# The split weight tiles of a one-core kernel placed behind the activations in SBUF

## The chip, the cores and the metric

One NeuronCore of a Trainium2 chip. The metric is the device time of one execution in microseconds (us); the median of three runs stands for a kernel.

## The reference, cut to what matters

Four residual half blocks and then a second block work on x, 256 tokens by 1024 features, in float32. What counts here is that nearly all of it is products of activations with weight matrices that are each used once:

```
h = rms_norm(x, g0);  x = x + rms_norm(mlstm_mixer(h), g1)        # w_in 1024 -> 3080, w_out 1024 -> 1024
h = rms_norm(x, g2);  x = x + rms_norm(relu(h @ w_up)**2 @ w_down, g3)   # 1024 -> 4096 -> 1024
... the same with short_conv_mixer (w_in 1024 -> 3072), and a second up/down
second block: x = x + [retention, pooling](norm(x) @ w_in) @ w_out
              x = x + softmax(q k^T / 16) v @ wo      # k, v from mem, 256 tokens by 1024
              x = x + (silu(gate) * val) @ w_down     # gate, val = conv3(norm(x) @ w_up), 1024 -> 5632, 2816 -> 1024
return rmsnorm(x, final_norm_g)
```

## The kernel before, in words

**Layout.** Activations are kept transposed: features on the 128 partitions, 8 chunks of them, 256 tokens along the free axis. Weights come from HBM as 159 slabs of 1 MB, each 128 x 2048 floats: 8 blocks of input features times 256 output columns.

For full precision each operand is split in a high part and a remainder: wH, wL for weights, xnH, xnL (normed activations), memH, memL (memory tokens), hH, hL (hidden layer of the MLPs) and mixH, mixL (mixer output) for activations. A product is three matmuls (`products`, L416 to L421): wH with the high activations, wH with the remainder, wL with the high ones. Per slab that is 8 blocks x 2 halves of columns x 3 = 48 matmuls, each 128 x 128 loaded against 128 x 256 streamed. The weight tile is the loaded operand, the activations stream:

```
pe.matmul(psum[:, n, 0:T], wH[w][:, wc], aH[:, ac, :], start=start, stop=False)     # L419: loads wH, streams aH
pe.matmul(psum[:, n, 0:T], wH[w][:, wc], aL[:, ac, :], start=False, stop=False)     # L420
return pe.matmul(psum[:, n, 0:T], wL[w][:, wc], aH[:, ac, :], start=False, stop=stop)  # L421
```

In ten slabs (v, rv and the fillers f4 to f7; `slab_by_token`, L438 to L448) it is the other way round: a 128 x 128 tile of the activations is loaded and 256 columns of wH or wL are streamed, so that tokens come out on partitions. In the names of the trace, `po<-xnH,wL` streams xnH and loads wL, and `po<-wL,xnH` streams wL and loads xnH.

**The stream of slabs.** SyncE loads slab s into raw[s % 4] as soon as the split of slab s - 4 is finished (`load`, L378). ScalarE copies each half slab to wH[s % 2] (`split`, L805), rounding it; VectorE writes wL = raw - wH (L1245), 318 instructions each. The write of wH for slab s waits until TensorE has finished the same half of slab s - 2. TensorE waits for each half's wL.

**The order of the work** is written out by hand in `PHASES` (L51): qk, v, o, out0, f4, f0, up0 (16 slabs), down0 (16), f1, cin (12), out1, f5, f2, up1, down1, f6, f3, rq, ru, rv, rg, out2, wq, f7, wo, fup (22), fdown (11). Where no number stands it is 4 slabs, or 2 for ru, rv and rg, or 1 for f0 to f7. The f slabs are fillers: products of the memory tokens with the keys' and values' weights, put where TensorE would otherwise wait for a norm. out0, out1, out2 and wo stream mixH and mixL; down0, down1 and fdown stream hH and hL; f0 to f3 stream memH and memL; all other slabs but the by-token ones stream xnH and xnL. Between the slabs' products TensorE does small work in plain fp32: sums of squares for the norms (L487), their spread over partitions (L494), head scores (L510, L511), attention scores (L721) and values (L743).

**The places in SBUF.** `sb` (L96) gives each tile the next free byte of every partition, in steps of 32, starting at the first multiple of 64 that is free (L94); in the program built here this is byte 16512, which is 128 past a multiple of 512. All residues in this document are counted mod 512 from that first byte, the start of raw0. The order of before is:

| tiles | bytes per partition | residue of each |
|---|---|---|
| raw0 to raw3 | 4 x 8192 | 0 |
| wH0, wH1, wL0, wL1 | 4 x 8192 | 0 |
| x, xnH, xnL, memH, memL, memk, memv | 7 x 8192 | 0 |
| ident, ones | 2 x 512 | 0 |
| par | 1312 | 0 |
| Rs, Rm, diag | 3 x 1024 | 288 |
| warm, ms, minus_half, rtok, rmem | 5 x 32 | 288 and up |
| scratch (y, squares, hrelu, hsq, apad, cgate, ...) | 16384 | 448 |
| region: hH, hL (32768 each), or mixH, mixL, qT, kT, xq, ... | | 448 for hH, hL, mixH, mixL, qT, kT, xq and xpT |

Every chunk of an activation tile is 1024 bytes and every block of weights 512, so each operand of a product starts at its tile's residue.

Of the kernel before, what the change touches and what calls it, by code (L numbers as in the profile page):

```python
# [2 lines left out]

# [6 lines left out]
P = 128  # L25
T = 256
TT = T // P
# [17 lines left out]
SLAB = 16 * P  # L45
HALF = SLAB // 2
RAW = 4
HL = 2
# [39 lines left out]
def build(nc, xT, memT, pos, weights, wgate, params, poolw, tri, mask, select, decay, freq, recount, out):  # L88
    f32, f32r, i32 = mybir.dt.float32, mybir.dt.float32r, mybir.dt.int32
# [3 lines left out]
    with ctx:  # L93
        place = [nc.sbuf_base + (-nc.sbuf_base) % 64]  # L94

        def sb(name, shape, dt, at=None):  # L96
            size = int(np.prod(shape[1:])) * 4
            if at is None:
                off = place[0]
                place[0] += (size + 31) // 32 * 32  # L100
            else:
                off = at[0]
                at[0] += (size + 31) // 32 * 32
            return nc.alloc_sbuf_tensor_at(name, list(shape), dt, offset=off)
# [3 lines left out]

        raw = [sb(f"raw{i}", [P, SLAB], f32) for i in range(RAW)]  # L110
        wH = [sb(f"wH{i}", [P, SLAB], f32r) for i in range(HL)]
        wL = [sb(f"wL{i}", [P, SLAB], f32r) for i in range(HL)]
        x = sb("x", [P, C, T], f32)
        xnH = sb("xnH", [P, C, T], f32r)
        xnL = sb("xnL", [P, C, T], f32r)
# [4 lines left out]
        ident = sb("ident", [P, P], f32)  # L120
        ones = sb("ones", [P, P], f32)
        par = sb("par", [P, NPAR], f32)
        Rs = sb("Rs", [P, T], f32)
        Rm = sb("Rm", [P, T], f32)
        diag = sb("diag", [P, TT, P], f32)
        warm = sb("warm", [P, 1], f32)
        ms = sb("ms", [P, TT], f32)
        minus_half = sb("minus_half", [P, 2 * NH], f32)
        rtok = sb("rtok", [P, TT], f32)
        rmem = sb("rmem", [P, TT], f32)  # L130
        scratch = place[0]
        at = [scratch]
        y = sb("y", [P, C, T], f32, at)
# [1882 lines left out]
```

## Time and profile before

| | |
|---|---|
| median of 3 runs | 1009.82 us (1009.44 to 1010.5) |
| span of the profiled execution | 1008.9 us, mean granted clock of TensorE 0.993 |
| TensorE busy (matmul, weight load) | 974.7 us (97%), 961.8 us (95%) |
| VectorE, ScalarE, POOL busy | 657.2 us (65%), 536.5 us (53%), 191.0 us (19%) |
| read from HBM | 170.24 MB |

The profile has the span alone (first to last instruction of one execution); its own total time is not recorded beside it, so the span stands against the median of the three other runs. Busy time of TensorE is of overlapping matmuls: a matmul's duration contains its way through the array, and the next one starts long before its end. A pace is therefore read from starts in the timeline.

### The profile page before, as it was taken

Reading aid. Unit: us, or ns where it says so; the run is one execution under the profiler, and the core shown is the slowest. Engines: PE = TensorE matmul, PEld = TensorE weight load, DVE = VectorE, ACT = ScalarE, POOL = GpSimd, SP = SyncE. Lnnn points to the kernel's source line nnn. Section 1 sums busy time; section 2 is a strip of 40 time slices with the busy share of each in tenths; the row PEclk is TensorE's granted clock in tenths of the full one; section 3 lists DMA queues with packets and bytes.
Section 4 is the critical chain, followed back from the end, with each engine's and each line's share of the span. In section 5 each row is a group of like instructions: output and inputs, shape, how many; then the busy total and the mean of one; then the engine's idle time right before and its main releaser. Section 6 shows DMA issues by size and latency. Waiting matters only on the chain.

```text
span 1008.9 us, 20181 instructions
## 1 busy us (share of the span) xinstructions
PE 974.7 (97%) x8062; PEld 961.8 (95%) x8062; DVE 657.2 (65%) x843; ACT 536.5 (53%) x754; POOL 191.0 (19%) x159
## 2 busy tenths in 40 slices
PE   7999989999999899999999999989999999999996
PEld 6999989999999799989999999889999999999995
DVE  6567586665444876577665444874865779999642
ACT  5566646554443544556555444554554566666541
POOL 2021140000010400149000010455120122223101
PEclk9999999999999999999999999999999999999997
DMA  9533635555555354535555553544342545555521
GB/s 342 183 126 112 216 131 188 190 171 204 186 189 172 123 206 168 189 129 190 196 173 198 182 205 137 196 159 168 128 166 86 181 152 177 197 191 183 205 88 42
DMA packets 25844, 172.17 MB, mean 171 GB/s; under 512 B 3252, under 2 KB 3892, under 8 KB 5432
## 3 DMA queue, kind: packets, MB, share of 16 engines
q1 hardware_dynamic: 25784, 171.30, 49.0%
q8 instruction: 46, 0.75, 0.3%
q14 instruction: 14, 0.11, 0.0%
HBM read 170.24 MB, written 1.05 MB: 170 GB/s over the span
## 4 chain that ended last, share of the span: by engine, by line
PE 85%; DVE 7%; issue 3%; POOL 2%; ACT 2%; DMA 1%; DVEq 0%; SPq 0%; ACTq 0%; POOLq 0%
PE po L419 25%; PE po L420 25%; PE po L421 25%; DVE xnL L1252 2%; DVE wL L1245 2%; PE po L446 2%; POOL rtok L1821 2%; PE po L448 2%; PE po L447 2%; PE pn L494 1%; ACT wH L805 1%; PE pn L487 1%; PE pc L743 1%; DMA raw<-in_weights 1%; DVE diag L1271 0%
## 5 line engine op out<-in xcount | busy, mean ns | idle before, releaser
L1245 DVE TENSOR_TENSOR wL<-raw,wH 128x1024 fp32r<-128x1024 f32 x318 | 404.0, 1294 | 157.8 <-ACT wH L805 157.8
L805 ACT ACTIVATE wH<-raw 128x1024 fp32r<-128x1024 f32 x318 | 334.8, 1059 | 295.5 <-PE po L421 264.8
L419 PE MATMUL po<-xnH,wH 128*128 128x256 f32 x1376 | 396.8, 288 | 18.9 <-DVE xnL L1252 13.2
L420 PE MATMUL po<-xnL,wH 128*128 128x256 f32 x1376 | 389.9, 283 | 0.0
L421 PE MATMUL po<-xnH,wL 128*128 128x256 f32 x1376 | 389.7, 283 | 0.0
L419 PEld LDWEIGHTS po<-xnH,wH 128*128 128x128 f32 x1376 | 264.3, 192 | 23.6 <-DVE xnL L1252 9.6
L420 PEld LDWEIGHTS po<-xnL,wH 128*128 128x128 f32 x1376 | 264.5, 192 | 0.2
L421 PEld LDWEIGHTS po<-xnH,wL 128*128 128x128 f32 x1376 | 264.4, 192 | 0.0
L419 PE MATMUL po<-hH,wH 128*128 128x256 f32 x688 | 189.9, 276 | 0.0
L420 PE MATMUL po<-hL,wH 128*128 128x256 f32 x688 | 189.9, 276 | 0.0
L421 PE MATMUL po<-hH,wL 128*128 128x256 f32 x688 | 189.9, 276 | 0.0
L1808 POOL TENSOR_TENSOR squares<-squares 128x512 f32<-128x512 f32 x26 | 39.7, 1528 | 525.0 <-ACT squares L853 368.7
L419 PEld LDWEIGHTS po<-hH,wH 128*128 128x128 f32 x688 | 129.1, 188 | 0.0
L420 PEld LDWEIGHTS po<-hL,wH 128*128 128x128 f32 x688 | 129.1, 188 | 0.0
L421 PEld LDWEIGHTS po<-hH,wL 128*128 128x128 f32 x688 | 129.1, 188 | 0.0
L419 PE MATMUL po<-mixH,wH 128*128 128x256 f32 x256 | 71.8, 280 | 0.5 <-DVE mixL L1287 0.5
L420 PE MATMUL po<-mixL,wH 128*128 128x256 f32 x256 | 71.0, 277 | 0.0
L421 PE MATMUL po<-mixH,wL 128*128 128x256 f32 x256 | 71.0, 277 | 0.0
L1512 DVE SCALAR_TENSOR_TENSOR hrelu<-po,Rs 128x512 f32<-128x512 f32 x32 | 22.1, 690 | 55.8 <-PE po L421 55.7
L1252 DVE SCALAR_TENSOR_TENSOR xnL<-x,par,xnH 128x256 fp32r<-128x256 f32 x56 | 48.6, 918 | 7.5 <-ACT xnH L819 7.5
L419 PEld LDWEIGHTS po<-mixH,wH 128*128 128x128 f32 x256 | 48.1, 188 | 0.9 <-DVE mixL L1287 0.7
L421 PEld LDWEIGHTS po<-mixH,wL 128*128 128x128 f32 x256 | 48.3, 189 | 0.0
(284 smaller groups left out, 1097.1 us busy)
## 6 DMA issues: line engine op xcount, KB each, us to landing
raw<-in_weights SPq DMA_DIRECT2D x158, 1024.0 KB, 4.8
x<-in_xT SPq DMA_DIRECT2D x4, 256.0 KB, 6.4
raw<-in_weights SPq DMA_DIRECT2D x2, 512.0 KB, 6.2
mem<-in_memT SPq DMA_DIRECT2D x1, 1024.0 KB, 12.6
out<-y SPq DMA_DIRECT2D x4, 256.0 KB, 2.4
decayt<-in_decay SPq DMA_DIRECT2D x1, 512.0 KB, 3.7
poolwt<-in_poolw SPq DMA_DIRECT2D x1, 256.0 KB, 3.7
par<-in_params SPq DMA_DIRECT2D x1, 164.0 KB, 3.4
```

What stands on the lines that cost most here:

```text
L419: pe.matmul(psum[:, n, 0:T], wH[w][:, wc], aH[:, ac, :], start=start, stop=False)
L420: pe.matmul(psum[:, n, 0:T], wH[w][:, wc], aL[:, ac, :], start=False, stop=False)
L421: return pe.matmul(psum[:, n, 0:T], wL[w][:, wc], aH[:, ac, :], start=False, stop=stop)
L446: pe.matmul(psum[:, t, 0:256], aH[:, k, tc], wH[w][:, wc], start=k == 0, stop=False)
L447: pe.matmul(psum[:, t, 0:256], aL[:, k, tc], wH[w][:, wc], start=False, stop=False)
L448: mm = pe.matmul(psum[:, t, 0:256], aH[:, k, tc], wL[w][:, wc], start=False, stop=k == 7)
L805: act.activation(wH[b % HL][:, hs], raw[b % RAW][:, hs], ACT.Copy).then_inc(s_hi, 1)
L1245: dve.tensor_tensor(wL[b % HL][:, hs], raw[b % RAW][:, hs], wH[b % HL][:, hs].bitcast(f32), ALU.subtract)\
L1252: k = dve.scalar_tensor_tensor(xnL[:, c, :], x[:, c, :], col(gain, c), xnH[:, c, :].bitcast(f32), ALU.mult, ALU.subtract)
L1512: dve.scalar_tensor_tensor(hrelu[n % 2][:, :, :], slot(GROUP0[up] + n)[:, :, 0:T], 0.0, over_pair(Rs[:, :]), ALU.max, ALU.mult).then_inc(s ...
L1808: pool.tensor_tensor(sq[0], sq[0], sq[p], ALU.add).then_inc(s_sqa, 1)
L1821: pool.tensor_tensor(r[:, :], ms[:, :], minus_half[:, 0:TT], ALU.pow).then_inc(s_r, 1)
```

## The change

The lines that allocate wH and wL move from behind raw to behind rmem, and Rs, Rm and diag move behind them. Nothing else in the program differs, apart from blank lines at the head of the file, which shift line numbers.

```
-        wH = [sb(f"wH{i}", [P, SLAB], f32r) for i in range(HL)]
-        wL = [sb(f"wL{i}", [P, SLAB], f32r) for i in range(HL)]
         x = sb("x", [P, C, T], f32)
...
         par = sb("par", [P, NPAR], f32)
-        Rs = sb("Rs", [P, T], f32)
-        Rm = sb("Rm", [P, T], f32)
-        diag = sb("diag", [P, TT, P], f32)
         warm = sb("warm", [P, 1], f32)
...
         rmem = sb("rmem", [P, TT], f32)
+        wH = [sb(f"wH{i}", [P, SLAB], f32r) for i in range(HL)]
+        wL = [sb(f"wL{i}", [P, SLAB], f32r) for i in range(HL)]
+        Rs = sb("Rs", [P, T], f32)
+        Rm = sb("Rm", [P, T], f32)
+        diag = sb("diag", [P, TT, P], f32)
         scratch = place[0]
```

Behind raw, whose end has residue 0, x to memv take 7 x 8192 bytes, ident and ones 1024, par 1312 and the five small tiles 160. So wH0 begins at residue 1024 + 1312 + 160 = 2496, which is 448 mod 512, and so do wH1, wL0, wL1, Rs, Rm and diag. x to par lie 32768 bytes lower, with the residues they had. The scratch and the region behind it stay at the same bytes.

| operands of the split products | slabs | loaded, streamed: before | after |
|---|---|---|---|
| weights loaded, xn or mem streamed | 90 | 0, 0 | 448, 0 |
| xn or mem loaded, weights streamed | 10 | 0, 0 | 0, 448 |
| weights loaded, hidden layer or mixer output streamed | 59 | 0, 448 | 448, 448 |

## Rows read from the trace of the kernel before

**Rows 1.** The page: span, busy time, and the chain that ended last by engine.
```profile
span 1008.9 us, 20181 instructions
PE 974.7 (97%) x8062; PEld 961.8 (95%) x8062; DVE 657.2 (65%) x843; ACT 536.5 (53%) x754; POOL 191.0 (19%) x159
...
PE 85%; DVE 7%; issue 3%; POOL 2%; ACT 2%; DMA 1%; DVEq 0%; SPq 0%; ACTq 0%; POOLq 0%
```

**Rows 2.** Waits: who waited for whom, us in total, times, longest us.
```profile
ACT wH L805 <- PE po L421: 264.8, 201, 4.4
...
PE po L419 <- DVE xnL L1252: 13.2, 11, 2.3
PE pn L494 <- DVE diag L1271: 3.9, 11, 1.6
```

**Rows 3.** Timeline of PE (start, us): a slab's ends in up1, down0, out2; v.
```profile
479.82 0.28 PE L419 MATMUL po<-xnH,wH 128*128 128x256 f32 x1
...
485.58 0.28 PE L419 MATMUL po<-xnH,wH 128*128 128x256 f32 x1
...
239.73 0.28 PE L419 MATMUL po<-hH,wH 128*128 128x256 f32 x1
...
245.17 0.28 PE L419 MATMUL po<-hH,wH 128*128 128x256 f32 x1
...
721.07 0.28 PE L419 MATMUL po<-mixH,wH 128*128 128x256 f32 x1
...
726.72 0.28 PE L419 MATMUL po<-mixH,wH 128*128 128x256 f32 x1
...
62.14 0.28 PE L447 MATMUL po<-wH,xnL 128*128 128x256 f32 x1
...
64.78 0.28 PE L448 MATMUL po<-wL,xnH 128*128 128x256 f32 x1
```

**Rows 4.** Windows (length, PE, PEld, DVE, ACT, POOL, PEclk): out0, up0, down0, fdown; fup's loop.
```profile
101.61:123.55 21.94, 21.94 (x196) 21.94 (x194) 13.33 (x14) 13.24 (x20) 3.33 (x3) 1.00 0.59 200
137.30:233.93 96.63, 94.27 (x778) 93.31 (x777) 63.81 (x73) 54.19 (x68) 7.69 (x6) 1.00 0.52 178
233.93:320.99 87.06, 87.06 (x771) 87.06 (x769) 41.78 (x35) 38.81 (x43) 3.33 (x3) 1.00 0.57 195
935.74:995.49 59.75, 59.75 (x530) 59.75 (x528) 28.76 (x29) 26.06 (x32) 5.94 (x5) 1.00 0.34 118
...
840.00:909.12 69.12, 69.12 (x579) 69.12 (x578) 66.72 (x86) 44.96 (x62) 18.66 (x14) 1.00 0.56 193
```

**Rows 5.** Groups by line and form: busy us, mean ns | idle before, releaser.
```profile
L1245 DVE TENSOR_TENSOR wL<-raw,wH 128x1024 fp32r<-128x1024 f32 x318 | 404.0, 1294 | 157.8 <-ACT wH L805 157.8
L421 PE MATMUL po<-xnH,wL 128*128 128x256 f32 x1376 | 389.7, 283 | 0.0
L421 PEld LDWEIGHTS po<-xnH,wL 128*128 128x128 f32 x1376 | 264.4, 192 | 0.0
L421 PE MATMUL po<-hH,wL 128*128 128x256 f32 x688 | 189.9, 276 | 0.0
L421 PEld LDWEIGHTS po<-hH,wL 128*128 128x128 f32 x688 | 129.1, 188 | 0.0
L420 PE MATMUL po<-memL,wH 128*128 128x256 f32 x64 | 18.1, 283 | 0.0
```

**Rows 6.** Small fp32 products: durations min/median/max ns by tile; the last from the timeline.
```profile
L510 PE MATMUL pc<-qT,kT x4: 377/377/378, 54.8 to 65.1; 128*128 128x256 f32 x4
L511 PEld LDWEIGHTS pc<-qT,kT x4: 188/188/189, 55.0 to 65.3; 128*128 128x128 f32 x4
L721 PE MATMUL pa<-memk,xq x16: 377/379/379, 752.7 to 766.0; 128*128 128x256 f32 x16
...
64.91 0.59 PE L510 MATMUL pc<-qT,kT 128*128 128x256 f32 x2
```

**Rows 7.** Groups of VectorE in fup's loop, 840 to 909.12 us.
```profile
L1245 DVE TENSOR_TENSOR wL<-raw,wH 128x1024 fp32r<-128x1024 f32 x26 | 39.4, 1554 | 0.0
```

## The prediction

> **What bounds the kernel now.** I read the page's busy shares first: TensorE works 97% of the span, VectorE 65%, ScalarE 53% [rows 1]. The chain that ended last agrees, with 85% of it on TensorE [rows 1], and TensorE's two largest sums of waits are 13.2 us, at the starts of stages whose activations are still being split, and 3.9 us [rows 2]. So the time is 7632 split products (159 slabs of 48), almost back to back, and the pace of one product decides. That pace can't be read from a mean duration, since matmuls overlap; the timeline gives it. From the first product of a slab to the first of the next there are 48 intervals: 485.58 - 479.82 = 5.76 us where xnH and xnL stream, 120.0 ns each; 245.17 - 239.73 = 5.44 us where hH and hL do, 113.3 ns [rows 3]. TensorE has the same granted clock, 1.00, in both stretches [rows 4], the same shapes and the same weight tiles. The groups by form repeat it: 283 ns for a matmul and 192 for a weight load with xn, 276 and 188 with hH [rows 5]. The by-token slabs, with activations loaded and weights streamed, also run at 120.0: 62.14 to 64.78 is 22 intervals [rows 3].
>
> What differs is the place. Residues below are mod 512 bytes, counted from the block's first tile. wH, wL, xnH, xnL, memH and memL lie at 0, while hH, hL, mixH and mixL lie at 448. So (loaded 0, streamed 0) costs 120.0 ns, (0, 448) 113.3, a difference of 6.67 ns. The four slabs of out2 are an exception: with (0, 448) they go at 726.72 - 721.07 = 5.65 us for 48, 117.7 ns, though out0 with the same tiles takes 21.94 us for 4 slabs, 5.49 each [rows 3, 4]. The pace then has at least three settled values, and residues alone don't choose between them.
>
> **The change part by part.** No instruction is added or removed, and no wait. (a) xnH, xnL, memH, memL streamed against weights now at 448: the pair is (448, 0), 4320 products in 90 slabs. (b) By-token slabs: (0, 448), the fast pair of today, 480 products in 10 slabs. (c) hH, hL, mixH, mixL: (448, 448), 2832 products in 59 slabs. (d) Rs, Rm and diag go from 288 to 448, and everything else keeps its residue. ScalarE writes and VectorE reads and writes the weight halves at another residue; the 318 splits of VectorE, 1294 ns each [rows 5], and as many copies of ScalarE have slack in all stages but one, where wH's next load waits 264.8 us in sum for TensorE [rows 2]. I cost (d) and this at nothing; without that cover each 10 ns on VectorE's 318 would be 3.2 us.
>
> The trace has no product with weights at 448, so I bound each pair from the nearest rows: 113.3 below and 120.0 above. The mechanism I take is that the two reads of TensorE disturb each other when both start at the same residue, and not otherwise: then (a) falls to 113.3, (b) as well, and (c) rises to 120.0. For: it is what separates the two populations, and the settled values hold for thousands of products whatever the other engines do. Against: the scores, both operands at 448, load kT in 188 ns at the median of L511 and stream in 377 [rows 6], no longer than memk at 0 against xq at 448 (379). But two of those products take 0.59 us from the first's start to the second's end [rows 6], so they start 0.59 - 0.38 = 0.21 us apart: longer than a load, which then bounds nothing, and they weigh little.
>
> Gain of (a) and (b), a slab giving 48 x 6.67 = 0.32 us where TensorE is never held:
> - up0, up1 and cin: 44 slabs, 14.1 us. VectorE is busy 63.8 of 96.6 us in up0 [rows 4], so it stays behind cover there; I keep 95%, 13.4.
> - fup: 22 slabs, 7.0 us at full rate. Here VectorE is busy 66.72 of 69.12 us, over 12 slabs [rows 4]: 5.56 us of work a slab, where TensorE would want 5.44. VectorE becomes the bound, and a slab saves 0.20 and not 0.32: 20 x 0.20 = 4.0, of which I take 3.0, since POOL's products (its tensor ops stretch the splits: 1554 ns here against 1294 overall [rows 5, 7]) come no sooner.
> - The other 34 slabs (qk, v, o, rq to rg, wq, and the eight fillers): 10.9 us at full rate. They hide norm chains, softmax and rotary work of the other engines, and a shorter cover leaves a longer wait behind it: the waits on xnL (11 of them, 13.2 us) and on diag (11, 3.9 us) [rows 2] would grow by what the slabs ahead save. I keep 60%, 6.5.
> Together 22.9 us, with 32.0 as upper end and some 16 (half) as lower.
>
> Loss of (c): down0, down1 and fdown are 43 slabs at 5.44 (59.75 / 11 = 5.43 [rows 4]), out0, out1 and wo 12, so 55 x 0.32 = 17.6; the 4 of out2 lose only 5.76 - 5.65 each, 0.4. TensorE is never idle there, so all 18.0 us count.
>
> Net -4.9 us on a span of 1008.9 [rows 1]. The three runs have a median of 1009.82, 0.9 us more than the profiled span, which I add: 1004.9, **1005 us**. The ends of this case are 1009.8 - 32.0 + 18.0 = 996 and 1009.8 - 16 + 18.0 = 1012.
>
> A rule speaks against any effect. The Trainium skill (SBUF — State Buffer, "Who interferes with whom") gives TensorE two independent read ports, one for the moving operand and one for weight loads, and says that TensorE never waits on anyone. By it placement is worth 0 and the sum stays 1009.8. Its sentence leaves 120.0 against 113.3 [rows 3] unexplained, so as far as it goes the trace does not agree.
>
> **The rivals.** What would measure as no change is within 0.2% (2.0 us).
> - *Settling between.* (a) ends in the 117.7 state of out2 [rows 3]: (c) costs 18.0, but (a) and (b) give 2.33 / 6.67 of 22.9, 8.0. 1009.8 + 10.0 = 1020, slower. For: fresh from a stop, that state caught (0, 448) once. Against: out0, with the same pair, runs at 5.49 us a slab [rows 4]. It turns slower as soon as the settled pace of (a) is above 114.8 ns (18.0 / 22.9 = 79% of 6.67 is needed to break even). 13%.
> - *One order only is good.* Fast needs the streamed tile 64 bytes behind the loaded one, as now with (0, 448); 64 ahead is as bad as level. (a) stays at 120.0, (c) rises by 18.0 us, and only (b) gains, 10 x 0.32 x 0.6 = 1.9: 1026, slower. 10%.
> - *Only the streamed tile's place counts.* 448 streamed is fast, whatever is loaded. (a) and (c) stay, (b) gains 1.9: 1008, on the edge of what can be measured. For: every fast product of the trace streams from 448, every slow one from 0, and kT's 188 ns with both at 448 [rows 6]. Against: no reason for a place to be bad by itself. 22%.
> - *The loaded tile at 448 is fast against anything.* (a) and (b) gain 22.9, (c) keeps 113.3: 987. Nothing in the rows has it but kT's 188 ns. 10%.
> - *Nothing.* High bytes or the tiles' history set the pace and the shift is empty: 1009.8. Against: memL lies 24 KB above xnH and has the same 283 ns [rows 5]. 5%. The rule of the Trainium skill named above leads here.
>
> **How the numbers follow.** The forecast has 40%. From it 33 points are faster, 5 within, 2 slower, since its own range runs from 996 to 1012. The streamed-place case splits 10 and 12, the loaded-place case is all faster (10), nothing is within (5), and the two slower cases are slower (23). Sum: faster 0.53, same 0.22, slower 0.25. The range runs from 998 to 1026; it leaves out the 987 case (10%) and the far end of the forecast.
>
> **What will show it.** Timeline of the profile after, 48 intervals of a slab: 5.44 us in up1 and 5.76 in down0 if I am right; by-token intervals at 113.3; fup at 5.55 to 5.6 a slab with VectorE busy 99% and TensorE waiting for wL; median loads 188 ns for xn and 192 for hH. Up at 5.76 and down at 5.44 would be the streamed-place case; up at 5.44 with down at 5.44 the loaded-place case; down at 5.76 without a gain in up one of the slower two. What would make me most wrong is a fourth settled value that (448, 0) has and no pair of today shows.

## The result: 0.6% slower, and the profile after

The kernel after takes 1016.0 us at the median of 9 runs (1013.10 to 1019.48), the kernel before 1009.91 in 9 runs beside it (1008.82 to 1012.91). The ratio is 1.0058, with a 95% interval of 1.0042 to 1.0075: slower, by nearly three times the 0.2% below which a difference would count as no change. The forecast was 1005 us, 0.5% faster.

The page of the kernel after: span, busy times of the engines, and the chain that ended last by engine.

```profile
span 1013.6 us, 20181 instructions
PE 980.2 (97%) x8062; PEld 967.2 (95%) x8062; DVE 660.7 (65%) x843; ACT 537.0 (53%) x754; POOL 187.7 (19%) x159
...
PE 84%; DVE 7%; issue 3%; POOL 2%; ACT 2%; DMA 1%; DVEq 0%; SPq 0%; ACTq 0%; POOLq 0%
```

Everything that [rows 1] showed is still so: the same number of instructions, the same busy shares, the same bound (TensorE has 84% of the chain in place of 85%). The span grew by 4.7 us. So the difference has to lie in the pace of the products. Below is the timeline of the kernel after, the two ends of one slab each in up0, down0, cin and up1 (columns: start us, duration us, engine, line, operation, tiles; 48 intervals lie between the two rows of a pair).

```profile
186.49 0.28 PE L404 MATMUL po<-xnH,wH 128*128 128x256 f32 x1
...
192.14 0.28 PE L404 MATMUL po<-xnH,wH 128*128 128x256 f32 x1
...
277.79 0.28 PE L404 MATMUL po<-hH,wH 128*128 128x256 f32 x1
...
283.55 0.28 PE L404 MATMUL po<-hH,wH 128*128 128x256 f32 x1
...
373.25 0.28 PE L404 MATMUL po<-xnH,wH 128*128 128x256 f32 x1
...
378.90 0.28 PE L404 MATMUL po<-xnH,wH 128*128 128x256 f32 x1
...
492.53 0.28 PE L404 MATMUL po<-xnH,wH 128*128 128x256 f32 x1
...
497.97 0.28 PE L404 MATMUL po<-xnH,wH 128*128 128x256 f32 x1
```

Down0 went from 5.44 to 5.76 us a slab, as forecast. Up0 and cin went from 5.76 only to 5.65, 117.8 ns a product, and up1 to the 5.44 that was forecast for all three, though it streams the same tiles against the same weights as up0. The stages tell the same in sum. Windows of the kernel after (length; busy us and count of PE, PEld, DVE, ACT, POOL; granted clock; DMA share; GB/s): out0, up0, down0, cin, up1, down1, fup, fdown, and the stretch in fup's loop.

```profile
99.64:122.86 23.22, 23.22 (x195) 23.16 (x194) 13.62 (x14) 13.50 (x20) 3.33 (x3) 1.00 0.56 195
136.48:231.71 95.23, 92.65 (x778) 91.67 (x777) 63.93 (x73) 54.27 (x68) 7.79 (x7) 1.00 0.53 180
231.71:323.87 92.16, 92.16 (x771) 92.16 (x770) 41.89 (x35) 38.72 (x43) 3.32 (x3) 1.00 0.54 186
333.57:407.17 73.60, 71.51 (x584) 71.01 (x585) 54.70 (x72) 37.14 (x49) 10.22 (x7) 0.95 0.47 160
443.55:536.05 92.50, 89.57 (x779) 88.61 (x777) 67.75 (x73) 54.44 (x69) 32.90 (x30) 1.00 0.54 184
536.05:628.20 92.15, 92.15 (x770) 92.15 (x769) 41.80 (x35) 40.73 (x46) 3.33 (x3) 1.00 0.49 169
810.43:937.24 126.81, 125.93 (x1066) 125.41 (x1065) 117.65 (x153) 81.43 (x111) 31.72 (x23) 1.00 0.52 179
937.24:1000.54 63.30, 63.30 (x530) 63.30 (x528) 30.48 (x33) 26.27 (x32) 5.92 (x5) 1.00 0.33 117
840.00:909.12 69.12, 69.12 (x590) 69.12 (x589) 67.38 (x88) 45.34 (x62) 17.78 (x12) 1.00 0.55 186
```

Against [rows 4], and against the same stages of before that no row there shows (up1 96.77, cin 74.56, fup 128.99, down1 87.06 us): down0 and down1 lose 5.1 each, fdown 3.6, the three outs and wo 1.3 + 1.1 + 0.4 + 1.1, together 17.6 us. Up0 gains 1.4, cin 1.0, up1 4.3, fup 2.2, v 1.1, and all the rest 2.9, together 12.9. The net is the 4.7 us by which the span grew; the 2.9 is what the other stages leave of it.

A part of cin's time is the clock's, whose mean is 0.95 there and 1.00 in the other stages. Windows of the kernel after over cin's start show where:

```profile
333.57:340.00 6.43, 4.58 (x23) 4.28 (x24) 6.43 (x9) 5.38 (x10) 4.75 (x4) 0.58 0.00 0
340.00:346.00 6.00, 6.00 (x49) 6.00 (x47) 3.48 (x4) 2.12 (x2) 3.85 (x3) 0.89 0.21 55
```

TensorE had waited 2.10 us for the split activations just ahead, and after its first products waits 1.85 more; the granted clock of 0.58 is mostly the lower level, 1.2 GHz, and from 346 us on it is 2.4 again. Before has a fall there too (0.98 over cin). At the lower level a product takes longer; these two rows of the kernel after have 15 intervals between them, 213.3 ns each:

```profile
337.89 0.41 PE L405 MATMUL po<-xnL,wH 128*128 128x256 f32 x1
...
341.09 0.41 PE L405 MATMUL po<-xnL,wH 128*128 128x256 f32 x1
```

Means over all products of a kind hide the two paces. Groups by form of the kernel after (count | busy us, mean ns | idle before):

```profile
L1230 DVE TENSOR_TENSOR wL<-raw,wH 128x1024 fp32r<-128x1024 f32 x318 | 411.1, 1316 | 168.6 <-ACT wH L790 168.5
L406 PE MATMUL po<-xnH,wL 128*128 128x256 f32 x1376 | 384.8, 280 | 0.0
L406 PEld LDWEIGHTS po<-xnH,wL 128*128 128x128 f32 x1376 | 260.0, 189 | 0.0
L406 PE MATMUL po<-hH,wL 128*128 128x256 f32 x688 | 194.7, 283 | 0.0
```

Against [rows 5], hH has taken the 283 ns that xnH had, and xnH has 280, between the 276 of hH and the 283 of xnH in the kernel before: a mixture. What TensorE waits for is hardly changed; waits of the kernel after (us in total, times, longest):

```profile
PE po L404 <- DVE xnL L1237: 12.6, 11, 2.1
PE pn L479 <- DVE diag L1256: 4.5, 11, 1.6
PE po L404 <- DVE wL L1230: 2.4, 3, 2.1
```

### The profile page after: what moved, and what is told of

The parts are those of the page before. It is cut to its first block, busy times and chain, and to the rows that moved or that the text cites. A ratio compares the mean times of both kernels' runs of the same rounds, so it can differ in the third digit from the quotient of the medians.

```text
span 1013.6 us, 20181 instructions
## 1 busy us (share of the span) xinstructions
PE 980.2 (97%) x8062; PEld 967.2 (95%) x8062; DVE 660.7 (65%) x843; ACT 537.0 (53%) x754; POOL 187.7 (19%) x159
## 4 chain that ended last, share of the span: by engine, by line
PE 84%; DVE 7%; issue 3%; POOL 2%; ACT 2%; DMA 1%; DVEq 0%; SPq 0%; ACTq 0%; POOLq 0%
PE po L404 25%; PE po L406 24%; PE po L405 24%; DVE xnL L1237 3%; DVE wL L1230 2%; PE po L431 2%; POOL rtok L1806 2%; PE po L432 2%; PE po L433 2%; PE pn L479 1%; ACT wH L790 1%; PE pn L472 1%; PE pc L728 1%; DMA raw<-in_weights 1%; DVE diag L1256 0%
## 5 line engine op out<-in xcount | busy, mean ns | idle before, releaser
L1230 DVE TENSOR_TENSOR wL<-raw,wH 128x1024 fp32r<-128x1024 f32 x318 | 411.1, 1316 | 168.6 <-ACT wH L790 168.5
L404 PE MATMUL po<-xnH,wH 128*128 128x256 f32 x1376 | 392.6, 285 | 17.7 <-DVE xnL L1237 12.6
L405 PE MATMUL po<-xnL,wH 128*128 128x256 f32 x1376 | 385.0, 280 | 0.0
L406 PE MATMUL po<-xnH,wL 128*128 128x256 f32 x1376 | 384.8, 280 | 0.0
L405 PEld LDWEIGHTS po<-xnL,wH 128*128 128x128 f32 x1376 | 259.9, 189 | 0.2
L406 PEld LDWEIGHTS po<-xnH,wL 128*128 128x128 f32 x1376 | 260.0, 189 | 0.0
L404 PE MATMUL po<-hH,wH 128*128 128x256 f32 x688 | 194.8, 283 | 0.0
L405 PE MATMUL po<-hL,wH 128*128 128x256 f32 x688 | 194.7, 283 | 0.0
L406 PE MATMUL po<-hH,wL 128*128 128x256 f32 x688 | 194.7, 283 | 0.0
L405 PEld LDWEIGHTS po<-mixL,wH 128*128 128x128 f32 x256 | 49.1, 192 | 0.0
```

Source lines behind the costliest of these rows:

```text
L1230: dve.tensor_tensor(wL[b % HL][:, hs], raw[b % RAW][:, hs], wH[b % HL][:, hs].bitcast(f32), ALU.subtract)\
```

## The experiments

In all that follows a pace is the mean time from the start of one product to the start of the next in a slab of 48, from the timeline; intervals of 130 ns and more (another product between, a wait) are left out. "Distance" is the residue of the streamed tile minus that of the loaded one, the shorter way round; a pair at distance 0 is called level. A "stop" is a place where TensorE starts no product for a while: it waits, or does small work of another kind in between. Before has distance 0 for xn and mem and -64 for h and mix; after has +64 and 0, and in its by-token slabs -64. Each kernel of this part was run with the kernel before beside it on the same chip, which took 1010.9 to 1011.3 us at the median. The ratios come from that comparison and are not exactly the quotient of the two medians.

**Is a level pair what costs, wherever the tiles lie?** Two kernels change the place of the scratch and of the region behind it alone, h and mix with them. The first starts from the kernel after; its h and mix go to residue 0 and so to +64:

```diff
+        place[0] += 64
         scratch = place[0]
```

> The changed kernel with 64 more bytes in front of the scratch: hidden layer and mixer output go from residue 448 to 0, weights stay at 448. Now both xn and h are streamed 64 bytes ahead (mod 512) of the loaded weights and nothing is level. Theory A (level start residues cost 120.0 ns a product; any other distance gives one of two settled paces, 113.3 or 117.8, picked at each stop of TensorE): the 59 slabs of h and mix leave 120.0 for a mixture of 113.3 and 117.8, so 6.5 to 18.9 us less than the 1016 of the changed kernel, 997 to 1010. Theory B (the order counts: 64 behind gives 113.3, 64 ahead 117.8): h and mix at 117.8 throughout, 1009 to 1010. Theory C (weights at 448 are slow against any tile but xn): h stays at 120.0 and the time at 1016.

Measured: 1011.52 us (999.79 to 1013.78, 10 runs), ratio to before 0.9981 (0.9949 to 1.0012). The 17.6 us are not all won back, because h and mix went from 120.0 to 117.8 and not to 113.3, in all seven stages. (Only the first 36 products of out1, entered from cin without a stop, held cin's 113.3; from the first stop on out1 too was at 117.8.) Timeline, a slab of down0 and one of cin:

```profile
277.39 0.28 PE L405 MATMUL po<-hH,wH 128*128 128x256 f32 x1
...
283.04 0.28 PE L405 MATMUL po<-hH,wH 128*128 128x256 f32 x1
...
369.65 0.28 PE L405 MATMUL po<-xnH,wH 128*128 128x256 f32 x1
...
375.09 0.28 PE L405 MATMUL po<-xnH,wH 128*128 128x256 f32 x1
```

Cin, untouched by this edit, ran at 113.3 here where the kernel after had 117.8. The second kernel does the same to the kernel before, so that h and mix are at distance 0 with the weights at their old place:

```diff
+        place[0] += 64
         scratch = place[0]
```

> The kernel before with 64 more bytes in front of the scratch and nothing else: hidden layer and mixer output go from residue 448 to 0, level with the weights at 0. This is the loss part of the change alone, at another absolute place. Theory A and B: 59 slabs at 5.76 us, 120.0 ns a product and the same in every execution, 18.3 us more than before, 1028. Theory C (it was the weights' place 448, not the distance, that slowed h): 113.3 stays, 1010. In between would speak against all three.

Measured: 1028.18 us (1027.20 to 1028.77, 4 runs), ratio 1.0176 (1.0159 to 1.0193). All stages settle at 120.0. Timeline, a slab of down0:

```profile
281.39 0.28 PE L420 MATMUL po<-hH,wH 128*128 128x256 f32 x1
...
287.15 0.28 PE L420 MATMUL po<-hH,wH 128*128 128x256 f32 x1
```

The same step of 64 bytes costs 1.76% in one kernel (1011.0 to 1028.2 us at the median) and wins in the other, where the ratio to before falls from the 1.0064 of the kernel after in this comparison (the next run) to 0.9981, and the median by 4.6 us. So neither a tile's own place nor a place of the loaded tile decides whether a pair is slow, but the distance. And distance 0 is at 120.0 in every stage of every profile: the loss of (c) is real and has this cause.

**Was 117.8 a matter of one execution?** The kernel after, unchanged, once more:

> The changed kernel once more, for a second profile of the same program. Theory A: h and mix at 120.0 again in every slab, but the stages of xn that sat at 113.3 (up1) and at 117.8 (up0, cin, fup) are others this time, and the time moves with them between 1013 and 1020. Theory B and any theory in which addresses alone choose the pace: up1 at 113.3 and up0, cin, fup at 117.8 again.

Measured: 1016.10 us (1012.44 to 1018.97, 4 runs), ratio 1.0064 (1.0041 to 1.0087), profiled span 1010.1. Timeline, a slab of cin:

```profile
370.96 0.28 PE L404 MATMUL po<-xnH,wH 128*128 128x256 f32 x1
...
376.40 0.28 PE L404 MATMUL po<-xnH,wH 128*128 128x256 f32 x1
```

Up0 is at 117.8 again, cin now at 113.3: its stage took 69.98 us, not 73.60, of which 12 slabs x 48 x 4.5 ns = 2.6 is the pace, and the granted clock is 1.00 over cin here in place of 0.95. The same program has another pace in the same stage. Those 3.6 us make up the difference of the two spans (3.5); fup won another 1.1 us (125.7 for 126.8), as its slabs 3 to 9 were at 113.3 here until a stop of 0.24 us at the start of slab 10 brought 117.8, and fdown lost the 1.1 again.

**Does the order count?** The kernel before with its small tiles moved ahead of x, so that x, xn and mem come to 448 with h and mix, and the weights stay at 0: every product by features is at -64, the by-token ones at +64.

```diff
+        ident = sb("ident", [P, P], f32)
+        ones = sb("ones", [P, P], f32)
+        par = sb("par", [P, NPAR], f32)
+        warm = sb("warm", [P, 1], f32)
...
         x = sb("x", [P, C, T], f32)
```

> The kernel before with ident, ones, par and the five small tiles allocated ahead of x: x, xn and mem go to residue 448, where h and mix are already, weights stay at 0. All 149 slabs that load weights stream 64 bytes behind them; the ten by-token slabs stream 64 ahead. Theory B: 113.3 nearly everywhere (out2's 117.8 an exception), VectorE bound in fup, about 22 us less than before, 987. Theory A: 113.3 in some stages and 117.8 in others, as the stops have it: between 987 and 1002 (all at 117.8 would save 8), and different from run to run by some us. If one order were bad by itself, as the rival of the prediction had it, xn at 64 behind would still give 987.

Measured: 1001.33 us (998.76 to 1011.16, 10 runs), ratio 0.9916 (0.9889 to 0.9943). It is faster than before, since nothing is level. Yet -64 is not simply the fast one: up0 went at 117.8 (95.2 us for the stage), and so did down0; fup was at 113.3 for 17 slabs and at 117.8 for its last five, again from a stop on. Timeline, a slab each of down0 and up1:

```profile
276.38 0.28 PE L419 MATMUL po<-hH,wH 128*128 128x256 f32 x1
...
282.03 0.28 PE L419 MATMUL po<-hH,wH 128*128 128x256 f32 x1
...
486.55 0.28 PE L419 MATMUL po<-xnH,wH 128*128 128x256 f32 x1
...
491.99 0.28 PE L419 MATMUL po<-xnH,wH 128*128 128x256 f32 x1
```

Down0 of this kernel has the pair that took 87.06 us before, and took 90.5. What differs is what came ahead: before, TensorE entered down0 without a stop from level products at 120.0; here it entered from up0 at 117.8, and stayed there. So, where nothing stops TensorE and the distance stays the same, the pace goes over from one stage to the next. In the kernel before, all of out1, down0, down1 and fdown were entered from level products without a stop, and all four settled at 113.3. The third value that out2 of before had [rows 3] is the same 117.8, there taken up right behind a stop.

**Which distances?** Four kernels shift x and everything behind it in the kernel before by one line ahead of x:

```diff
+        place[0] += 256
         x = sb("x", [P, C, T], f32)
```

and the same with 128, 32 and 192.

> The kernel before with 256 bytes left free between wL and x: weights at 0, xn and mem at 256, hidden layer and mixer output at 192. Theory A (only level is slow, every other distance has the same two paces): no 120.0 anywhere, stages at 113.3 or 117.8 as the stops have it, so 997 to 1005 and a spread of several us between executions, like the kernel with the activations at 448. Theory D (the distance sets more than level or not): one pace throughout, either 113.3, which gives 987 with VectorE bound in fup, or another value than the three known.

Measured: 1010.98 us (1010.16 to 1012.45, 10 runs), ratio 1.0002 (0.9991 to 1.0012). Timeline, a slab of up0 and one of down0:

```profile
187.59 0.28 PE L420 MATMUL po<-xnH,wH 128*128 128x256 f32 x1
...
193.35 0.28 PE L420 MATMUL po<-xnH,wH 128*128 128x256 f32 x1
...
277.21 0.28 PE L420 MATMUL po<-hH,wH 128*128 128x256 f32 x1
...
282.65 0.28 PE L420 MATMUL po<-hH,wH 128*128 128x256 f32 x1
```

At 256 the old picture is back, 120.0 and 113.3, so distances count mod 256 and not mod 512: 256 acts as level, and 192, where h and mix are now, acts as -64 did.

> The same with 128 bytes: xn and mem at 128, hidden layer and mixer output at 64. Theory A: 113.3 or 117.8 in every stage, 997 to 1010. Theory D: xn at a pace of its own, and h (64 ahead) at 117.8 as with the scratch moved by 64, so the two kinds of stages differ in a fixed way.

Measured: 1017.77 us (1016.07 to 1020.70, 4 runs), ratio 1.0054 (1.0035 to 1.0073). Here xn is at 128 and goes at 118.7 in most stages and at 120.0 in up0 and fup; h and mix at +64 go at 117.8 in all.

> The same with 32 bytes: xn and mem at 32, hidden layer and mixer output at 480, 32 behind. It asks how wide level is. If two reads disturb each other only when they start at the same residue, 32 is as good as 64: 113.3 or 117.8, 997 to 1010. If what they share is a unit of 64 bytes or more, xn at 32 stays level with weights at 0 and costs 120.0 (90 slabs), while h at 480 lies in the unit behind and keeps 113.3: 1008 to 1011, as before.

Measured: 1013.64 us (1012.56 to 1014.88, 10 runs), ratio 1.0025 (1.0015 to 1.0035): xn at +32 at 116.7, in fup at 117.8; h and mix at -32 at 118.3.

> The kernel before with 192 bytes between wL and x: xn and mem at 192, hidden layer and mixer output at 128. With 256 bytes xn ran at 120.0 as if level, and h at 192 at 113.3 as before. If what counts is the distance mod 256, then 192 ahead is 64 behind: xn at 113.3 or 117.8 by the stops, and h and mix at the 118.7 that 128 gave to xn, in every slab. 59 slabs cost 59 x 48 x 5.4 ns = 15.3 us more than before and 100 slabs give 8 to 22.9: 1003 to 1018. If 512 is the period and 256 was a second bad place, xn may be anything, and h at 128 need not show 118.7.

Measured: 1013.07 us (1009.61 to 1014.39, 10 runs), ratio 1.0015 (1.0003 to 1.0026). Xn at 192, -64 mod 256, has the two paces of -64: 113.3 in up1, 117.8 in up0, cin and fup. H and mix at 128 have 118.7 in out0, down1, out2 and wo, and 120.0 in down0 and out1. No distance tried is better than 64 at its better pace, and all four kernels of this group are slower than the one with the activations at 448.

**What resets the pace?** If level products lead to 113.3 when -64 follows them, some can be put in on purpose. The kernel with the activations at 448 again, but with the last of the 8 chunks of xnH and xnL in tiles of their own ahead of the small ones, at residue 0: in each slab with xn 42 products are at -64 and 6 are level.

```diff
+        class Chunks:
...
+            def __getitem__(self, at):
+                p, c, t = at
+                return self.last[p, t] if c == C - 1 else self.first[p, c, t]
+
+        xnH7 = sb("xnH7", [P, T], f32r)
+        xnL7 = sb("xnL7", [P, T], f32r)
...
+        xnH = Chunks(sb("xnH", [P, C - 1, T], f32r), xnH7)
+        xnL = Chunks(sb("xnL", [P, C - 1, T], f32r), xnL7)
```

> The kernel with the activations at 448, but the last of the eight chunks of xnH and xnL has a place of its own at residue 0, level with the weights: 6 products of each xn slab cost 120.0 on purpose. In the kernel before all six stages of h and mix that were entered from level products, without a stop between, settled at 113.3. If level products reset the pace, every slab of xn after the first of a stage starts fast: 42 at 113.3, 6 at 120.0 and some 18 ns until it has settled, 114.6 on average, in every stage and every execution; h and mix enter from it and stay at 113.3; VectorE bounds fup. 993 to 999, and a spread under 3 us where the kernel with the activations at 448 had 12. If the pace after a stop is held through level products, 42 of 48 stay at 117.8: 118.0 on average in such stages, 1000 to 1010.

Measured: 995.22 us (994.74 to 996.47, 4 runs), ratio 0.9841 (0.9823 to 0.9858). Timeline of this kernel, a slab of up1, then its windows of up0, down0, up1, down1, fup and fdown:

```profile
481.38 0.28 PE L429 MATMUL po<-xnH,wH 128*128 128x256 f32 x1
...
486.86 0.28 PE L429 MATMUL po<-xnH,wH 128*128 128x256 f32 x1
```

```profile
136.93:229.74 92.81, 90.12 (x778) 89.17 (x777) 63.93 (x73) 54.25 (x68) 7.79 (x7) 1.00 0.53 184
229.74:316.80 87.06, 87.06 (x771) 87.06 (x769) 41.78 (x35) 38.81 (x43) 3.33 (x3) 1.00 0.56 196
432.35:525.22 92.87, 90.16 (x778) 89.21 (x777) 67.26 (x73) 54.29 (x68) 32.83 (x30) 1.00 0.52 184
525.22:612.28 87.06, 87.06 (x771) 87.06 (x769) 41.70 (x35) 40.70 (x46) 3.34 (x3) 1.00 0.50 179
792.47:917.31 124.84, 123.79 (x1066) 122.91 (x1065) 115.77 (x154) 78.21 (x110) 31.83 (x23) 1.00 0.51 183
917.31:979.50 62.19, 60.31 (x530) 59.92 (x528) 32.09 (x33) 27.43 (x34) 6.88 (x6) 1.00 0.35 119
```

A slab with xn takes 5.48 us: (42 x 113.3 + 6 x 120.0) / 48 = 114.1 ns, measured 114.2. The downs enter from there and have 87.06 us, as before. Fdown doesn't come back to its 59.75 us [rows 4], though its slabs settle at 113.3: PE is busy 60.31 of 62.19 us here. The timeline of this kernel has one wait there, for VectorE's wL, at the start of fdown's third slab:

```profile
930.53 0.38 PE L429 MATMUL po<-hH,wH 128*128 128x256 f32 x1 [1.85 <-DVE wL L1255]
```

The kernel before has no such wait in fdown. Five of the 14 profiles ran a part of fup at 113.3 or 114.2, and all five have more than 1 us between two starts at this place (1.2 to 2.1); the other nine have 0.34 at most. So VectorE falls behind while TensorE runs faster through fup, and part of what fup wins is paid here.

Fup also shows the reset at work. At the start of its slab 12 stands a short stop, and 117.8 behind it; the 6 level products that end the slab are followed, without a stop, by 113.3 (intervals in ns, worked out from the timeline; the bar stands where slab 13 begins):

```
119 117 118 118 117 118 122 116 119 119 121 116 | 119 121 116 114 114 113 113 114 113 113
```

In the two profiles of this kernel (the second is below) six slabs with xn at 117.8 ended in 6 level products without a stop behind them, and all six were followed by 113.3.

The same trick on the other side, in the kernel with h apart (weights at 448): the last chunks level with the weights at 448, all else at +64.

```diff
+        xnH = Chunks(xnH8, sb("xnH7", [P, T], f32r))
+        xnL = Chunks(xnL8, sb("xnL7", [P, T], f32r))
...
+        place[0] += 64
         scratch = place[0]
```

> The changed kernel with h and mix moved to residue 0 (64 bytes ahead of the weights at 448, as xn is), and with the last chunk of xnH and xnL at 448, level with the weights. It is the mirror image of the kernel with the last chunk at 0 and the rest at 448: the same kick, but the other tiles stream 64 ahead and not 64 behind. If only the distance's size counts and level products reset the pace to 113.3, xn slabs average 114.6 and h and mix stay at 113.3: 993 to 999. If 64 ahead is another case than 64 behind and settles at 117.8 after level products (h at 64 ahead was at 117.8 in all but a few products of two profiles), xn slabs average 118.0 and h 117.8: 1009 to 1013.

Measured: 1014.14 us (1013.01 to 1015.26, 7 runs), ratio 1.0032 (1.0021 to 1.0044). Timeline, a slab of up1:

```profile
491.18 0.28 PE L415 MATMUL po<-xnH,wH 128*128 128x256 f32 x1
...
496.86 0.28 PE L415 MATMUL po<-xnH,wH 128*128 128x256 f32 x1
```

The slab of up1 takes 5.68 us, (42 x 117.8 + 6 x 120.0) / 48 = 118.1 ns a product, and h and mix are at 117.8 everywhere. So the order does count: behind level products -64 settles at 113.3, and +64 at 117.8. Most of the 19 us between this kernel and the one with level chunks and -64 are this. The two kernels differ in one thing more, as the weights lie at 448 in one and at 0 in the other; that this place doesn't matter is argued and not shown. The kernel with 128 bytes between speaks for it: its h and mix are at +64 with the weights at 0 and went at 117.8 in all stages, though not behind level products.

With the last chunk of xnL alone level (2 products of 48, one at a time), and xnH whole at -64:

```diff
+        xnL = Chunks(sb("xnL", [P, C - 1, T], f32r), xnL7)
```

> The kernel with the last chunk level, but of xnL alone: xnH lies whole at 448, xnL's last chunk at 0. Two products of each xn slab are level in place of six, three products apart. If one level product is enough to reset the pace, a slab averages (46 x 113.3 + 2 x 120 + some 10) / 48 = 113.8 and the time is 1 to 2 us under the 995.2 of six level products, 993 to 995. If two single ones don't do it, stages that came out of a stop at 117.8 stay there: 1000 to 1008, with the spread of the kernel without level products.

Measured: 998.76 us (994.75 to 1003.30, 6 runs), ratio 0.9874 (0.9845 to 0.9903). Up0 held 117.8 from its third slab to its end and took down0 with it (90.5 us), while cin and up1 settled at 114.3 and down1 at 113.3. In none of the 26 places of this profile where a slab with xn at 117.8 went over into the next without a stop did the pace come down. Single level products don't reset it.

The kernel with both last chunks level, once more:

> The kernel with six level products once more, beside the one with two, for the interval against the kernel before and a second profile. The pace of an xn slab should again be 114.2 to 114.6 after the first of each stage, and that of h and mix 113.3 wherever they are entered from such a slab: 994 to 997, ratio to before 0.984.

Measured: 996.25 us (995.52 to 998.35, 4 runs), ratio 0.9858 (0.9841 to 0.9876). It repeats: up0, cin and up1 at 114.2, both downs, out1, out2 and wo at 113.3. Fdown took 63.8 us: the wait for wL is there again (1.83 us), and behind it the granted clock was 0.58 for 3 us. It is the fastest of the study, faster than both kernels, and its runs lie within 3 us, where those of the kernel with the activations at 448 spread over 12.

The paces by stage, worked out from the timelines, ns; the pace held by the end of the stage. For fup of the two kernels with level chunks at -64 it is the median of the slabs from the third on, since TensorE stops there again and again; in the first of them slabs 12, 14, 16 and 18 were at 118.0.

```
                      distance xn   up0    cin    up1    fup    distance h   out0   down0  down1  fdown
before                     0       120.0  120.0  120.0  120.0     -64       113.3  113.3  113.3  113.3
after                    +64       117.8  117.8  113.3  117.8       0       120.0  120.0  120.0  120.0
after again              +64       117.8  113.3  113.3  117.8       0       120.0  120.0  120.0  120.0
h apart                  +64       117.8  113.3  117.8  117.8     +64       117.8  117.8  117.8  117.8
h level                    0       120.0  120.0  120.0  120.0       0       120.0  120.0  120.0  120.0
activations at 448       -64       117.8  113.3  113.3  117.8     -64       113.3  117.8  113.3  117.8
gap 192                  -64       117.8  117.8  113.3  117.8     128       118.6  120.0  118.7  120.0
level chunks, -64     -64 and 0    114.2  114.2  114.2  114.2     -64       117.8  113.3  113.3  113.3
the same again        -64 and 0    114.2  114.2  114.2  114.2     -64       113.3  113.3  113.3  113.3
level chunks, +64     +64 and 0    118.2  118.2  118.2  118.2     +64       117.8  117.8  117.8  117.8
```

## Why the prediction was wrong

**What held.** The bound (TensorE's stream, at a pace to be read from starts) held, and a pair at the same residue is slow, as the h-level and the h-apart kernels show. That it is the two reads of TensorE that disturb each other fits all runs, but none of them shows the reads themselves. The loss of (c) was forecast at 18.0 us and measured 17.6, out2's smaller share included (0.4 and 0.4). (b), the by-token slabs at -64, went to 113.7 to 114.1 in v, where 113.3 was forecast. (d) and the engines' other accesses cost nothing that shows: VectorE's split went from 1294 to 1316 ns on average, with no more waiting of TensorE for wL (3.3 us in sum before, 2.4 after). The h-level kernel has 1315 with the weights at their old place, so the new place isn't what stretched it.

**The step that failed** is the settled pace of (a), 4320 of the 7632 products. The prediction bounded it by 113.3 and 120.0 and took the lower end, on the reasoning that an undisturbed pair has one pace. It has two, 113.3 and 117.8. Up0, cin and fup held 117.8, only up1 113.3. At 117.8 a slab saves 48 x 2.2 = 0.11 us and not 0.32: up0 should then save 1.7 us (measured 1.4), cin 1.3 (1.0), fup 2.3 (2.2), and up1 at 113.3 for 14 of its 16 slabs 4.5 and a little for the first two (4.3). For these four the prediction had 13.4 + 3.0 = 16.4, and the runs gave 8.9. Of the other 34 slabs it had 6.5, and they gave 4.0. The total is 12.9 in place of 22.9, under the 18 that the loss asks for.

**Fup's bound.** The forecast made VectorE the bound of fup at 5.56 us a slab. In the kernel after TensorE went at 5.65, so VectorE was not reached: it was busy 67.38 of 69.12 us and TensorE all of it. Where the pace did fall, with level chunks, fup's slabs 4 to 11 took 5.48 to 5.51 us, less than VectorE's 5.56, so VectorE had work in hand; from slab 12 on they took 5.62 on average. Fup as a whole took 124.8 us, 4.2 less than before, near the 3 to 4 that the prediction allowed it. But 2.4 of these came back in fdown, 62.2 us for 59.75, with TensorE waiting for wL, and the prediction had no term for that.

**The rivals.** *Settling between* is the one that came true, for most of (a); it gave 1020 with all of (a) at 117.7, and the kernel lies below it as up1 was at 113.3. The evidence was there: out2's four slabs at 5.65 with the fast pair [rows 3], which the prediction called an exception. As the only settled pace of the trace that the mechanism didn't explain, it deserved more than the 13% it got. *One order only is good* is half right: +64 is not as bad as level, but behind level products it is worse than -64. *Only the streamed tile's place* and *the loaded tile at 448* fell with down0, at 120.0 with both at 448, and *nothing* with the time itself.

**The rule of the Trainium skill** (SBUF — State Buffer, "Who interferes with whom"), by which TensorE's two read ports are independent and TensorE never waits on anyone, would make every one of these kernels take the same time. They reach from 995.2 to 1028.2 us on the same instructions (20181 in each profile). The trace doesn't agree, and the measurement decides: for an fp32r product with its own weight load, in this stream, the distance of the two addresses costs up to 6.7 ns on top of 113.3.

**What stays open.** Why there are two paces at the same distance, and what in a stop of TensorE picks one, no run shows. Why 6 level products reset the pace at -64 and not at +64 is open too. I also didn't try two orders of the three products, or a load that serves more than one product, either of which would change how reads overlap.

## What to carry to other kernels

Where TensorE loads weights for every product, look at the start residues mod 256 of what it loads and what it streams: in this kernel level was never good, the streamed tile 64 bytes behind was best, and 6 level products in each slab of 48 held the better pace. A pace that is read off one stage of a trace can be inherited from the stage ahead, so check what the stage begins from. And where one stretch of the trace doesn't fit the mechanism, give the case that the rest behaves like it a chance of weight. And move a shared tile only after pricing all of its partners: here 59 slabs lost the good distance so that 100 could leave the bad one.

## What the runs showed of the hardware that I had not expected

- The distance counts mod 256: 256 goes as 0 (120.0 ns), 192 as -64 (113.3 or 117.8).
- The pace is chosen after a stop of TensorE and held. These are the first intervals of four stretches of products, ns, worked out from the timelines. Out0 of before, up1 and up0 of after are shown from their last stop on; down0 of before follows level products without one:

```
before, out0  (-64)     114 123 119 113 113 114 113 113 ...
after,  up1   (+64)     114 113 113 114 113 113 114 113 ...
after,  up0   (+64)     117 116 122 117 118 118 118 117 ...
before, down0 (-64)     120 121 121 116 114 114 113 ...
```

  After at most a dozen products the value stands (4 or fewer at -64). In the 14 profiles no stretch without a stop, at distance 0, -64 or +64, changed its pace after that; the longest at -64 is 1451 products at 117.8 (activations at 448, up0 into f1). A later stop can choose anew, also in the middle of a stage, and a very short one does: in up1 of after, 117.8 gave way to 113.3 where one start came 166 ns behind the last. Of the stretches of 24 products and more that began behind a stop, some 70% took 113.3 at -64 (99 of 139), but only one in six at +64 (16 of 97).
- The choice varies between executions of one program, as the two profiles of the kernel after show. That goes with spread in the time of a kernel: runs of the kernel after reach over 6.4 us (9 runs), of h apart over 14.0 (10), of activations at 448 over 12.4 (10); with xn level and h at -64 (256 between) over 2.3 (10), with all products level (h level) over 1.6 (4), and with the pace brought back in every slab over 1.7 and 2.8 (4 each). That the pace is all of this spread is argued: only one execution of each run has a profile.
- Distance 128 has two paces as well, 118.7 and 120.0; at +32 stand 116.7 and 117.8, at -32 118.3.
- At the lower clock level the distance made no difference. The stretches with a granted clock at 1.2 GHz, 11 to 18 intervals each, have 213.2 to 213.7 ns a product at distance 0 (before, cin), +64 (after, cin), -64 (level chunks again, cin and fdown) and 128 (gap 128, cin) alike.
